# Moving the streamed weight tiles of a two-layer diffusion block from 64-byte to 32-byte starts in SBUF

## The reference

```python
for i in range(DEPTH):                       # DEPTH = 2
    sh1, sc1, g1, sh2, sc2, g2 = _ada(c, ada_w[i], ada_b[i])      # silu(c) @ (2048 x 12288)
    hx = _modulate(_rmsnorm(x, norm1_g[i]), sh1, sc1)
    yx = _mla(hx, hc, ...) if i == 0 else _fourier_mix(hx, fno_w[0])
    x = x + g1 * yx
    x = x + g2 * _conv_ffn(_modulate(_rmsnorm(x, norm2_g[i]), sh2, sc2),
                           ffn_w_up[i], ffn_conv_w[i], ffn_conv_b[i], ffn_w_down[i])
return _rmsnorm(x, final_norm_g)

def _conv_ffn(h, w_up, conv_w, conv_b, w_down):      # D_FF = 5632
    u = _dwconv3(h @ w_up, conv_w, conv_b)
    val, gate = jnp.split(u, 2, axis=-1)
    return (val * jax.nn.silu(gate)) @ w_down
```

## The kernel before, in words

| tile | start before | remainder by 64 |
|---|---|---|
| `x`, `h_hi`, `h_lo` (`h_pre` at the place of `h_lo`) | 0, 16384, 32768 | 0 |
| (64 bytes left free, line 102) | 49152 | |
| `raw` (and `early`), `ada` | 49216, 65600 | 0 |
| `w_hi`, `w_lo`, `acc0` | 81984, 98368, 114752 | 0 |
| `rstd`, `sq`, `sqt`, `conv_s`, `const_s`, `mod` to `lgain_s` | 122944 to 133504 | 0 |
| `scl`, `cond_s`, `silu_c`, `silu_s`, `negmax`, `rinv` | 133536 to 134432 | 32 |
| (32 bytes left free, line 133) | 134496 | |
| `phase_at`: the tiles of each stage (`ckv`, `cq`, heads, `a_hi`, `a_lo`, `cv`, `f_hi`, `acc1`, `dft`) | 134528 on | 0 |

## Time and profile before

### The profile page before, as it was taken

How to read it: one execution, slowest core, us unless ns; L and a number is a source line. 1 busy time by engine, 2 the same in 40 slices (tenths; PEclk the granted TensorE clock), 3 DMA queues, 4 the chain that set the end, 5 groups by cost and what they waited for, 6 DMA issues and landing times.

```text
span 2242.4 us, 46076 instructions
## 1 busy us (share of the span) xinstructions
PE 2158.3 (96%) x17426; PEld 2079.0 (93%) x17426; DVE 1712.4 (76%) x1955; ACT 1150.2 (51%) x1527; POOL 177.7 (8%) x128
## 2 busy tenths in 40 slices
PE   7898999998899999999999999979999999999997
PEld 3577999898899999999999999979999999999997
DVE  6866887888988888788778876988886664456665
ACT  6874554433666666433345443346666663334542
POOL 0000000046000000000000230720000000000013
PEclk9999999998999999899999999989999999999999
DMA  9853665678588887699967752958776555555553
GB/s 348 310 213 108 221 227 204 222 283 337 187 290 294 289 288 282 250 372 372 371 217 288 279 209 75 359 207 295 282 248 201 189 196 186 190 195 185 182 186 122
DMA packets 127799, 547.01 MB, mean 244 GB/s; under 512 B 14576, under 2 KB 15088, under 8 KB 107248
## 3 DMA queue, kind: packets, MB, share of 16 engines
q1 hardware_dynamic: 127728, 546.03, 67.6%
HBM read 543.88 MB, written 2.10 MB: 243 GB/s over the span
## 4 chain that ended last, share of the span: by engine, by line
PE 83%; DVE 12%; issue 2%; ACT 1%; DMA 1%; POOL 0%; DVEq 0%; SPq 0%; ACTq 0%; POOLq 0%
PE bank L1280 24%; PE bank L1281 24%; PE bank L1282 24%; DVE acc L808 3%; PE bank L1311 2%; DVE w_lo L785 2%; PE bank L1345 2%; DVE w_lo L840 1%; PE bank L1286 1%; PE bank L1287 1%; PE bank L1288 1%; DMA ada<-ada_late 1%; PE bank L1331 1%; PE bank L1362 1%; PE bank L1361 1%
## 5 line engine op out<-in xcount | busy, mean ns | idle before, releaser
L485 ACT CAST w_hi<-raw 128x1024 fp32r<-128x1024 f32 x624 | 652.4, 1050 | 536.3 <-PE bank L1282 457.8
L785 DVE TENSOR_TENSOR w_lo<-raw,w_hi 128x1024 fp32r<-128x1024 f32 x624 | 771.4, 1248 | 181.0 <-ACT w_hi L485 180.5
L1280 PE MATMUL bank<-h_hi,w_hi 128*128 128x256 f32 x3152 | 880.9, 279 | 14.4 <-DVE w_lo L785 9.9
L1281 PE MATMUL bank<-h_lo,w_hi 128*128 128x256 f32 x3152 | 878.9, 279 | 0.0
L1282 PE MATMUL bank<-h_hi,w_lo 128*128 128x256 f32 x3152 | 878.8, 279 | 0.0
L1280 PEld LDWEIGHTS bank<-h_hi,w_hi 128*128 128x128 f32 x3152 | 599.4, 190 | 15.4 <-issue 15.2
L1281 PEld LDWEIGHTS bank<-h_lo,w_hi 128*128 128x128 f32 x3152 | 597.5, 190 | 0.3 <-issue 0.2
L1282 PEld LDWEIGHTS bank<-h_hi,w_lo 128*128 128x128 f32 x3152 | 597.1, 189 | 0.0
L1280 PE MATMUL bank<-a_hi,w_hi 128*128 128x256 f32 x1408 | 393.4, 279 | 1.7 <-DVE a_lo L789 1.7
L1281 PE MATMUL bank<-a_lo,w_hi 128*128 128x256 f32 x1408 | 393.1, 279 | 0.0
L1282 PE MATMUL bank<-a_hi,w_lo 128*128 128x256 f32 x1408 | 392.5, 279 | 0.0
(11 more groups left out here) (199 smaller groups left out, 2456.7 us busy)
## 6 DMA issues: line engine op xcount, KB each, us to landing
raw<-weights SPq DMA_DIRECT2D x626, 512.0 KB, 4.7
ada<-ada_late SPq DMA_DIRECT2D x160, 1024.0 KB, 5.0
early<-weights SPq DMA_DIRECT2D x72, 512.0 KB, 5.3
kv_raw<-kv_weights SPq DMA_DIRECT2D x8, 512.0 KB, 6.4
ctx_s<-ctxT SPq DMA_DIRECT2D x4, 512.0 KB, 5.3
x<-xT SPq DMA_DIRECT2D x4, 512.0 KB, 8.4
outT<-h_pre SPq DMA_DIRECT2D x4, 512.0 KB, 2.6
dft_s<-dft SPq DMA_DIRECT2D x1, 768.0 KB, 7.7
```

Source lines behind the costliest of these rows:

```text
L485: act.copy(w_hi[:, slot, :], raw[:, slot, :]).then_inc(hi_done, 1)
L785: dve.tensor_tensor(w_lo[:, slot, :], raw[:, slot, :], w_hi[:, slot, :].bitcast(f32), ALU.subtract)\
L1280: pe.matmul(out, wh, hi_part, start=first, stop=False)
L1281: pe.matmul(out, wh, lo_part, start=False, stop=False)
```

## The change

In the first free gap 32 bytes are left in place of 64, and the gap of 32 bytes ahead of `phase_at` goes. All tiles from `raw` to `warm` then start 32 bytes earlier: those that were at multiples of 64 are now 32 bytes past one (`raw` and `early` at 49184, `ada`, `w_hi`, `w_lo`, `acc0` and the rest likewise), and the small ones from `scl` on that were 32 bytes past one are now at multiples of 64. `phase_at` moves by 64 bytes, to 134464, so the tiles of the stages stay at multiples of 64. `x`, `h_hi`, `h_lo` and `h_pre` stay where they are. No instruction is added, removed or moved on any engine, and sizes and access patterns stay.

```diff
@@ -99,7 +99,7 @@
         h_at = cursor[0]
         h_lo = place("h_lo", [P, KT, SEQ], f32r)
         h_pre = at("h_pre", [P, KT, SEQ], f32, h_at)
-        cursor[0] += 64
+        cursor[0] += 32
         early = at("early", [P, EARLY_RING, CH], f32, cursor[0])
         raw = place("raw", [P, RING, CH])
         ada = place("ada", [P, ARING, D])
@@ -130,7 +130,6 @@
         rinv = place("rinv", [P, 2])
         warm = place("warm", [P, 1])
         ident, ones = const_s[:, 0, :], const_s[:, 1, :]
-        cursor[0] += 32
         phase_at = cursor[0]
```

## The result

The changed kernel took 2292.57 us in the median of four runs (2290.47 to 2293.94; 21 executions on record reach from 2283.96 to 2300.82), the kernel before 2253.35 us in four (2244.2 to 2261.51). The ratio is 1.0169, with a 95% interval of 1.0142 to 1.0196: slower by 39 us. The profiled execution of the changed kernel took 2292.81 us, its span is 2291.0 us, 48.6 us over that of before. The lines of the program quoted here have numbers one lower than before.

The account below looks back on a forecast made before the run. The prediction took TensorE to bound the kernel, busy 96% of the span and 83% of the chain. All terms were put at 0, so the sum was 0 and the forecast 2252 us, with a range of 2236 to 2290 us.

Parts of the forecast that it names:

- rival 2: TensorE: loading the stationary block becomes the step; slower by 115 us, 2367 us, decided at 5 ns more per load; chance 0.07.
- Stationary operand: TensorE's 13,680 loads out of `w_hi` and `w_lo`: odd starts cost 0, upper end 115 us.
- the different starts give no second level: TensorE loads of `silu_s` at multiples of 16 bytes: 81 to 128 ns, median 85, so cost taken as 0.
- Is there room to hide one more?: TensorE load, one more 64-byte piece: 108 ns per load against a step of 113.3 ns leaves 5 ns of room.
- The upper end, 115 us: TensorE loads: one more eighth of 108 ns, 13.5 ns, less the room of 5: 8.4 ns times 13,680.
- Moving operand: TensorE: `a_hi`, `a_lo`, `f_hi` move by 64 bytes; equal steps of 113.3 and 113.4 ns, so cost 0.
- rival 1: Stages with DMA share 0.93 and over: traffic landing at odd starts costs more; 15 to 26 us slower; chance 0.24.
- rival 3: Near-full DMA stages: the new lie of the rows disturbs TensorE less; 15 us go, 2237 us; chance 0.15.
- the 15 us: Matmuls slowed in near-full DMA stages: 8.9 us down-projection of layer 0, 3.9 Fourier square, 2.0 `wo`; could double or go.
- the inference from the earlier trace: VectorE and ScalarE: odd starts cost 0, from line 1147 against line 1150, 480 and 483 ns; bounds 18 and 10 us busy.
- 2958 matmuls again in the stretch of layer 1's up-projection: Sign that the forecast is right: TensorE's step stays at 113.3 ns in layer 1's up-projection.

Follow-up runs that it names:

- first experiment: The changed kernel with `w_hi` and `w_lo` alone put back on multiples of 64, `raw`, `ada` and `acc0` still at odd starts: ratio to before 0.998, median 2259.54 us.
- the scan: Small kernel of TensorE alone: twelve layouts with weights at multiples of 64 from the moving operand, nine bursts of 96 matmuls each; steps 113.3 to 120.8 ns.

## Why the prediction was wrong

The forecast was 2252 us with a range to 2290; the time was 2292.57. The direction was one of its rivals'.

**The steps that failed.** The sum's terms for TensorE's operands, both put at 0, together with the price that the prediction gave to rival 2. *Stationary operand*: "the different starts give no second level" rested on the earlier trace rows, loads of four columns that never meet the moving operand in the pattern of the product, and "Is there room to hide one more?" treated the load as work of its own length. The runs show a property of the pair. The upper end, 115 us, had the right place and sign; where it reckoned 8.4 ns for each load, measured it is at most 5.0 ns where before had 113.3 (up-projections), 3.3 ns in layer 1's down-projection, and between -1.1 and 0.6 where before was in its slow mode. (One stretch of some 20 us went from 113.3 to 117.8.) From 460 us on the mean step at full clock went from 114.7 to 117.8 ns over some 14,000 matmuls: 43 of the 48.6 us. *Moving operand*: "a move by a multiple of 64 costs nothing" rested on two tiles that both happened to show 113.3 in the earlier trace rows; `a_hi` had it at a distance at which most stretches have 117.8. Leaving out 64 bytes costs 2.8%, adding 128 costs 1.1%.

**The reading that misled.** From the earlier trace rows it took the DMA share for the cause of the slower step, and built rival 1 and rival 3 on it. The trace of before contradicts it in both directions, in `wo` at a full share and in the last down-projection at a light one:

```profile
505.00:515.00 10.00, 10.00 (x90) 1.00 0.94 358
2190.00:2200.00 10.00, 10.00 (x87) 1.00 0.59 193
```

The first has the fast step of 113.3 ns and the second the slow one of 117.8. The 115.9 ns of `wo` was that fast step with a few late starts and a clock of 0.98, and the 119.1 ns of the down-projection the step of 117.8 with a clock of 0.99. So the 15 us that rival 1 doubles and rival 3 gives back weren't the traffic's. The rival had the direction of the result, but its mechanism was wrong: raw's rows at odd starts cost nothing (first experiment), and neither does full traffic. The Trainium skill's statement that engines and DMA don't slow each other ("SBUF — State Buffer", "SBUF: two separate sides") was set aside for a false reason. No run here speaks against it, and the kernel with 128 bytes between the weight tiles agrees: 1238 matmuls in 140 us, the fast step, at a DMA share of 1.00.

**What held.** VectorE and ScalarE cost nothing at odd starts: their durations agree within 0.3%, and the inference from the earlier trace rows came out. For DMA no cost shows: the share stayed within the 67 to 68% that the prediction named, and the 1.9% more packet time came without odd starts too. "2958 matmuls again in the stretch of layer 1's up-projection" failed (2369 in 280 us where before had 2473), and it was named as the sign of rival 2: "a step over 115 ns in stages where DMA is light". The sign was right and pointed at the right engine.

**What stays open.** Why a distance by 256 bytes sets TensorE's step, what chooses between 113.3 and 117.8 ns when a stretch starts, and why the full kernels reached 113.3 at a distance of 192 where 18 bursts of the scan never did, no run shows.

## What to carry to other kernels

In a loop bound by TensorE in which a load and a matmul alternate, look at the step between matmul starts, in several stages, and against more than one suspect: two discrete values that each last from 20 to over 300 us, and runs that spread by 1 to 2%, point to a mode and not to traffic. Addresses are then a free knob: vary the distance of the stationary tile from the moving one by 32 to 256 bytes, high and low parts apart, in a small kernel of TensorE alone, and put the best into the full one. Alignment of each tile for itself, even to 128 bytes, says nothing. All this was measured for float32r blocks of 128 loaded and 256 moving columns; for other types and sizes no run shows it.

## What the runs showed of the hardware

TensorE's step for 128 loaded and 256 moving float32r columns at full clock, by the distance of the weights from the moving operand, remainder by 256 bytes (high and low tiles at the same remainder). "Alone" is the small kernels, "kernel" the full ones:

| distance | alone, ns | kernel, ns |
|---|---|---|
| 0 | 120.0 | 120.0 |
| 32 | 118.3 | 118.3 |
| 48, 68, 80 | 117.8 (one 123.3), 118.3, 118.7 | |
| 64 | 113.3 or 117.8 | 113.3 or 117.8 |
| 96 | 117.3 or 118.7 | 117.3 or 118.7 |
| 128 | 118.7 or 120.0 | 118.7 or 120.0 |
| 160 | | 120.0 |
| 192 | 117.8 | 117.8, in four stretches 113.3 |
| 224 | | 116.7, once 117.8 |
| 64 high, 192 low | 113.3 | 113.3 |

The small kernel and the full one agree in each row that both have, though the full one has DMA, ScalarE and VectorE at work. The exception is 192: two stretches of before (from 1294 us and the down-projection of layer 1) and two of the kernel with the weights put back (from 1295 us and the Fourier square) had 113.3, where 18 separate bursts at 192 and 448 never had it. Coming from a stage at 113.3 isn't enough for it: the down-projection of layer 0 in before did, and stepped at 117.8. With no loss of speed the DMA engines filled `raw` and `ada` at 386 GB/s beside TensorE at its fastest step.
